# Two transformer blocks on one core: all attention issued beside projections, one score block ahead, and 64-row score matmuls issued in alternating pairs

## The reference

```python
# first block, mixer of one layer
a_in, b_x, b_b, b_c, q, k, v, gate_in = split_cols(h @ w_in[l], IN_SPLITS)
br_a = multiscale_pool(a_in, pool_w[l], pool_scale[l]) @ w_branch_a[l]
br_b = (b_b * causal_dwconv(b_c * b_x, conv_b_w[l])) @ w_branch_b[l]
q = apply_partial_rope(q.reshape(b, s, ATTN_HEADS, HEAD_DIM), cos, sin)   # 12 heads of 64
k = apply_partial_rope(k.reshape(b, s, ATTN_HEADS, HEAD_DIM), cos, sin)
br_c = dilated_attention(q, k, v) @ w_branch_c[l]       # 3 groups, one softmax over them
merged = gates[:, :, 0] * br_a + gates[:, :, 1] * br_b + gates[:, :, 2] * br_c
x = x + rmsnorm(merged @ w_out[l], norm_mix_post[l])
# memory attention, 4 heads of 128, 256 keys: softmax(q k^T / sqrt(128)) v
# second block, layer 0: 8 query heads and 2 key heads of 64 in a window, with a sink; and
outs = [einsum('bhqk,bkhd->bqhd', p[:, 0] - lam * p[:, 1], v) for p, (_, v) in zip(probs, kv_parts)]
# (4 heads, two softmax maps of 64 rows each, values 128 wide)
# second block, layer 1: 16 heads, scores over 64 + 32 rows, values 64 wide, 768 keys
```

## Time and profile before

| | |
|---|---|
| median of 3 runs | 4576.96 us (4574.52 to 4582.12) |
| the profiled execution's own time | 4583.58 us |
| its span | 4581.8 us |
| TensorE (PE) busy | 4184.2 us, 91% of the span |
| weight loads (PEld) | 3461.2 us, 76% |
| DVE, ACT, POOL busy | 1836.9, 1392.0, 1419.6 us |
| mean granted TensorE clock | 0.916 of full speed |

### The profile page before, as it was taken

How to read it: one execution, slowest core, us unless ns; L and a number is a source line. 1 busy time by engine, 2 the same in 40 slices (tenths; PEclk the granted TensorE clock), 3 DMA queues, 4 the chain that set the end, 5 groups by cost and what they waited for, 6 DMA issues and landing times.

```text
span 4581.8 us, 48460 instructions
## 1 busy us (share of the span) xinstructions
PE 4184.2 (91%) x19548; PEld 3461.2 (76%) x19548; DVE 1836.9 (40%) x3065; ACT 1392.0 (30%) x2044; POOL 1419.6 (31%) x644
## 2 busy tenths in 40 slices
PE   6899998999989999999988888889999879989998
PEld 4778767777668776767767777779999668876886
DVE  4433445654643243574454444341111544433113
ACT  3223334332322233433223333231111323343222
POOL 2213533655431254355541000112222200003442
PEclk9877999999997799999989988799999877789999
DMA  2211332444321133234431000012221100002332
GB/s 91 66 42 58 113 92 69 127 126 129 99 75 37 51 111 101 64 118 126 126 109 28 19 19 19 24 42 64 61 64 56 47 14 13 12 25 72 94 94 77
DMA packets 544827, 317.85 MB, mean 69 GB/s; under 512 B 35876, under 2 KB 517599, under 8 KB 544607
## 3 DMA queue, kind: packets, MB, share of 16 engines
q1 hardware_dynamic: 544335, 313.71, 23.4%
q10 hardware_dynamic: 272, 1.05, 0.1%
HBM read 312.62 MB, written 2.10 MB: 69 GB/s over the span
## 4 chain that ended last, share of the span: by engine, by line
PE 80%; DVE 12%; ACT 3%; issue 2%; POOL 1%; DMA 1%; SPq 0%; PEld 0%; DVEq 0%; PEldq 0%; ACTq 0%
PE acc L452 23%; PE acc L454 22%; PE acc L453 22%; PE ob L1058 3%; PE pt L1033 2%; PE ob L868 2%; PE ob L1310 2%; POOL wlo L436 1%; PE pt L862 1%; DVE small L1145 1%; DVE t L701 1%; DVE t L2169 1%; DVE t L592 1%; PE pt L688 1%; DVE hl L607 1%
## 5 line engine op out<-in xcount | busy, mean ns | idle before, releaser
L436 POOL TENSOR_TENSOR wlo<-wraw,whi 128x1024 fp32r<-128x1024 f32 (+5 forms) x640 | 1419.4, 2224 | 3126.6 <-ACT whi L429 3125.6
L452 PE MATMUL acc<-hh,whi 128*128 128x512 f32 (+4 forms) x3320 | 1297.6, 391 | 88.7 <-DVE hl L607 32.6
L454 PE MATMUL acc<-hh,wlo 128*128 128x512 f32 (+4 forms) x3320 | 1254.2, 378 | 0.0
L453 PE MATMUL acc<-hl,whi 128*128 128x512 f32 (+4 forms) x3320 | 1251.5, 377 | 0.0
L429 ACT ACTIVATE whi<-wraw 128x1024 fp32r<-128x1024 f32 (+5 forms) x640 | 625.0, 980 | 999.6 <-DMA wraw<-in_ada_w 269.0
L452 PEld LDWEIGHTS acc<-hh,whi 128*128 128x128 f32 (+1 forms) x3320 | 637.9, 192 | 243.2 <-issue 82.8
L453 PEld LDWEIGHTS acc<-hl,whi 128*128 128x128 f32 (+1 forms) x3320 | 638.3, 192 | 110.6 <-issue 17.9
L454 PEld LDWEIGHTS acc<-hh,wlo 128*128 128x128 f32 (+1 forms) x3320 | 636.1, 192 | 95.3 <-issue 0.2
L1439 DVE TENSOR_TENSOR t<-acc,sq 128x768 f32<-128x768 f32 (+1 forms) x44 | 36.3, 824 | 501.7 <-PE acc L454 501.7
L454 PE MATMUL acc<-act1h,wlo 128*128 128x512 f32 x528 | 209.5, 397 | 0.0
L1096 ACT ACTIVATE sq<-pt 128x768 f32<-128x768 f32 (+1 forms) x136 | 95.1, 699 | 375.2 <-PE pt L1033 375.1
(11 more groups left out here) (352 smaller groups left out, 6069.4 us busy)
## 6 DMA issues: line engine op xcount, KB each, us to landing
wraw<-in_ffn_w SPq DMA_DIRECT2D x120, 512.0 KB, 3.8
wraw<-in_w_in SPq DMA_DIRECT2D x102, 512.0 KB, 3.8
wraw<-in_ada_w SPq DMA_DIRECT2D x96, 512.0 KB, 4.0
wraw<-in_w_up SPq DMA_DIRECT2D x88, 512.0 KB, 4.0
wraw<-in_w_down SPq DMA_DIRECT2D x32, 512.0 KB, 4.3
wraw<-in_w_out SPq DMA_DIRECT2D x16, 512.0 KB, 4.0
wraw<-in_w_mkv SPq DMA_DIRECT2D x16, 512.0 KB, 4.0
wraw<-in_ab_w_in SPq DMA_DIRECT2D x14, 512.0 KB, 3.8
```

Source lines behind the costliest of these rows:

```text
L436: e.tensor_tensor(wlo[0:rows, s, a:b, 0:w], wraw[0:rows, s, a:b, 0:w], whi[0:rows, s, a:b, 0:w].bitcast(F32), ALU.subtract).then_inc(lo_re ...
L452: e.matmul(o, wh, xh, start=first, stop=False)
L453: e.matmul(o, wh, xl, start=False, stop=False)
L454: return e.matmul(o, wl, xh, start=False, stop=last)
```

## The change

The functions for attention alone, for attention beside projections, and for tiles of projections become one family, `pe_flow`, `act_flow` and `dve_flow`. It takes a list of iterations, a list of jobs (slabs and small steps with them) and a list of ticks, which says which part of which job runs in which iteration. Either list may be empty; with no iterations (`wide`) the jobs use the four slots of `acc0` and `acc1`. With iterations the scores take both `acc`, PV has `ob[0]` alone and the slab has `ob[1]`, one bank, so a slab for 768 tokens becomes one of 512 and one of 256. TensorE's order in tick n is: scores of n+1, transposes of a finished slab of values, transposes of n, PV of n-1, part of a slab.

Where a head is 64 rows wide (the first block, window attention, both maps of differential attention), two neighbours' score matmuls are issued in turn, one from partitions 0 to 63 and one from 64 to 127, into `acc0` and `acc1`:

```diff
+                if its[n].get("pair"):
+                    if n % 2:
+                        return
+                    side = [(n, 0), (n + 1, 0)]
+                for k, m in side:
+                    b = its[k]["s"][m]
+                    if used[b] is not None:
+                        masked, i = used[b]
+                        e.wait_ge(s_nb if masked else s_probs, c.at(s_nb if masked else s_probs, i + 1))
+                    used[b] = (its[k]["mask"] is not None, first[k] + m)
+                pieces = len(its[n]["maps"][0])
+                for p in range(pieces):
+                    for x in range(3):
+                        for k, m in side:
+                            q_hi, q_lo, k_hi, k_lo, at = its[k]["maps"][m][p]
+                            mm = e.matmul(scores_of(its[k], m)[:, at:at + k_hi.shape[-1]], q_lo if x == 2 else q_hi,
+                                          k_lo if x == 1 else k_hi, start=x == 0, stop=x == 2)
+                            if p == pieces - 1 and x == 2:
+                                mm.then_inc(s_scores, 1)
...
+            for n in range(-1, max(N + 1, len(ticks))):
+                tick = ticks[n + 1] if n + 1 < len(ticks) else None
+                over_ = jobs[before[0]] if ends(before) else dict(kind="")
+                vt = over_ if over_["kind"] in ("v", "kv") else None
+                raws += vt is not None
+                fulls += over_["kind"] in ("kv", "feat") or over_["kind"] == "plain" and not over_.get("rx")
+                if n + 1 < N:
+                    ready(its[n + 1]["need"])
+                    scores(n + 1)
+                if vt and not (wide and tick):
+                    values(vt)
+                if 0 <= n < N:
+                    t = its[n]
...
+                if 1 <= n <= N:
+                    t = its[n - 1]
+                    ready(t.get("need_v", t["need"]))
+                    e.wait_ge(s_copied, c.at(s_copied, n))
+                    e.wait_ge(ob_free[0], c.next(ob_free[0]))
+                    slot["pv"] = n
+                    for j, vj in enumerate(t["v"]):
+                        mm = e.matmul(ob[0][:, 0:t["dv"]], sq[:, 0, j * P:j * P + P], vj, start=j == 0,
+                                      stop=j == len(t["v"]) - 1)
+                    mm.then_inc(s_pv, 1)
                 if tick:
                     part(tick)
```

In a mixer of the first block pooling and convolution slabs move behind the slabs of queries, keys and values, beside the attention: 7 slabs with the 8 iterations of j = 0, 6 with those of j = 1. The loads on SP move with them:

```diff
-                ws, s = weights(e, c), c.turn("slab")
-                claim(e, c, s, TC)
-                take(e, c, [pt_free])
-                e.wait_ge(pool_ready, c.next(pool_ready, 4))
+                pe_flow(e, c, [], tiles_1(0), one_each(tiles_1(0)), hh, hl, wide=True)
+                pe_flow(e, c, its_1(0), jobs_1(0), ticks_1(0), hh, hl)
+                pe_flow(e, c, [], tiles_1(1), one_each(tiles_1(1)), hh, hl, wide=True, extra=(0, lambda: done_1(e, c, 0)))
+                pe_flow(e, c, its_1(1), jobs_1(1), ticks_1(1), hh, hl)
...
-                mm.then_inc(slab_done, 1)
-
-                for j in range(2):
-                    pe_tiles(e, c, tiles_1(j), K8, hh, hl)
-                    pe_attention(e, c, its_1(j))
-                    pe_features(e, c, ot1, 1, 4)
-                    feats = c.next(feat_ready, view="slab")
...
+                heads(0)
+                for g in range(4):
+                    load(e, c, [(0, P, rows_of(w_in, l, 0, KT, g * PG, PG))], PG)
+                conv(0)
+                heads(1)
+                conv(1)
+                conv(2)
```

The rotary turn is now a partition shuffle on DVE everywhere (before, only in the second block's streams); the matmul with the permutation is gone, and the lo part of tile i is taken by DVE before tile i+1's turn is begun. A convolution step or a pooling step is a job on DVE in its tick:

```diff
+                M, T, w, u = j["M"], j["T"], j["work"], j["t"]
+                src = jbank(s)[0:M, 0:T]
+                if j.get("rx"):
+                    st(e.tensor_tensor(j["raw"][0:M, 0:T], src, rstd[0:M, 0:T], ALU.mult))
+                    jrelease(e, s)
+                    src = j["raw"][0:M, 0:T]
+                e.tensor_tensor(w[0:M, 0:T], src, rope_c[0:M, 0:T], ALU.mult).then_inc(dve_step, 1)
+                e.stream_shuffle(u[0:M, 0:T], src, j["swap"]).then_inc(dve_step, 1)
+                e.wait_ge(dve_step, c.next(dve_step, 2))
+                if not j.get("rx"):
+                    jrelease(e, s)
+                st(e.tensor_tensor(u[0:M, 0:T], u[0:M, 0:T], rope_s[0:M, 0:T], ALU.mult))
+                e.tensor_tensor(w[0:M, 0:T], w[0:M, 0:T], u[0:M, 0:T], ALU.add).then_inc(s_sum, 1)
...
+                elif j["kind"] == "conv1":
+                    st(e.tensor_tensor(halves(zc[:, i % 2, PAD:]), halves(jbank(s)), bx(i), ALU.mult))
+                    jrelease(e, s)
+                    st(e.tensor_scalar(w, zc[:, i % 2, PAD:], wcol(2), None, ALU.mult))
+                    for k in (1, 0):
+                        st(e.scalar_tensor_tensor(out=w, in0=zc[:, i % 2, PAD - 2 + k:PAD + SEQ - 2 + k], scalar=wcol(k),
+                                                  in1=w, op0=ALU.mult, op1=ALU.add))
+                    st(e.tensor_tensor(w, w, rstd[:, 0:SEQ], ALU.mult))
```

More of the change, by code:

```diff
@@ L972, in instances, with ends @@
             return first, n
[L974 to L995 removed]
+        def ends(tick):
+            return tick and tick[3]
@@ L1000, in part @@
                 if k0 == 0:
[L1001 to L1009 removed]
+                    if t.get("fetch", True) and t["kind"] != "feat":
+                        slot["work"] = weights(e, c)
@@ new lines, in part @@
+                    slot["was"] = slot.get("s")
+                    if wide:
+                        slot["s"] = c.turn("slab")
+                        claim(e, c, slot["s"], SEQ)
+                    else:
+                        slot["s"] = None
+                        e.wait_ge(proj_free, c.next(proj_free))
+                    if t.get("stats"):
+                        e.wait_ge(pt_free, c.next(pt_free))
+                s = slot["s"]
+                if t["kind"] == "feat":
+                    e.wait_ge(ob_free[0], c.at(ob_free[0], 1 + t["after"] - slot.get("pv", 0)))
+                    for r in range(4):
+                        mm = e.transpose(jbank(s)[:, r * P:r * P + P], t["src"][:, r, :], ident[:, :])
+                    mm.then_inc(s_job, 1)
+                    return
@@ L1106, in act_stream @@
-                if tick and tick[3]:
-                    j = jobs[tick[0]]
-                    head(e, c)
-                    s, done = c.turn("acc"), c.next(slab_done)
-                    if j["kind"] != "rope":
-                        e.wait_ge(slab_done, done)
-                        e.activation(v3(sq[:, 1, 0:j["T"]], j["T"]), bank(s, j["T"], j["M"]), ACT.Copy).then_inc(s_raw, 1)
+                    if n == N:
+                        e.wait_ge(s_copied, c.next(s_copied, N))
+                        e.sem_inc(pt_free, 1)
@@ new lines, in act_flow @@
+                if n + 1 < N:
+                    exps(n + 1)
+                    combs += len(its[n + 1]["maps"]) == 2
+                if ends(before):
+                    j = jobs[before[0]]
+                    if j["kind"] in ("rope", "pool", "conv2") or j["kind"] == "plain" and j.get("rx"):
+                        sums += 1
+                        e.wait_ge(s_sum, c.at(s_sum, sums))
+                        e.activation(j["hi"], j.get("arrange", same)(j["work"][0:j["span"], 0:j["T"]]), ACT.Copy).then_inc(s_hi, 1)
@@ L1210, in dve_stream @@
+            before = None
+            for n in range(-1, max(N + 2, len(ticks))):
+                tick = ticks[n + 1] if n + 1 < len(ticks) else None
+                if n + 1 < N:
+                    for m in range(len(its[n + 1]["maps"])):
+                        maxima(n + 1, m)
+                if 0 <= n - 2 < N:
                     result(n - 2)
-                if before and before[3]:
+                if ends(before):
                     j, s = jobs[before[0]], slots[before[0]]
-                    if j["kind"] != "v":
+                    if j["kind"] in ("rope", "pool", "conv2") or j["kind"] == "plain" and j.get("rx"):
@@ L1645, in swap, with both @@
-        def swap(block, half):
-            return [p + half if p % block < half else p - half if p % block < 2 * half else p for p in range(32)]
+                         dst=otm[:, r, a * P:a * P + P], s=(r % 2,), need=needs[a][0], need_v=needs[a][1])
+                    for a in range(4) for r in range(4)]
+        all_tok = [slice(i * P, i * P + P) for i in range(4)]
+        def both(kind, hi, lo, **more):
+            return [dict(more, kind="rope", span=more["M"], T=SEQ, hi=hi[:, 0:SEQ], lo=lo[:, 0:SEQ], done=False),
+                    dict(more, kind="plain", span=more["M"], T=CTX, c0=SEQ, hi=hi[:, SEQ:TC], lo=lo[:, SEQ:TC], fetch=False)]
```

1042 lines of the change are left out of this document (437 added, 605 removed).

## The result

The changed kernel takes 4627.93 us (median of 4 runs, 4617.35 to 4629.0) against 4579.34 of the kernel before on the same chip: the ratio is 1.0102, 95% interval 1.0084 to 1.012. It is 1% slower, where 6% faster was forecast. Its profiled execution has a span of 4627.2 us.

What follows compares the result with a forecast made beforehand. TensorE, busy 91% of the span, was taken as the bound: its work divided by its clock. Gains 98 + 16 + 75 + 72 + 5 = 266 off 4583.6 gave 4317.6, less 6.6 about 4310 us; range 4200 to 4440.

Steps and rivals of the forecast that it cites:

- The two waits it has every iteration ... go: Differential attention, layer 0 of the second block: waits for ACT's exponential (0.73 us) and DVE's combination (0.44) vanish.
- The text's own warning: Sign of being wrong: DVE stands between TensorE and its accumulators in more than the rotary tiles; no size given.
- First-block mixers: Two first-block mixers: each falls from 341.9 to 292.7 us, a gain of 49, 98 for both.
- lateness of rotary tiles: First-block mixers: rotary tiles, paced by DVE and ACT, take 8.2 us each, 2.6 late; 18 us a mixer (4 to 24).
- Memory attention: Memory attention: its idle 8.2 us is covered by eight slabs that move in; 8 a layer, 16 gained (0 to 25).
- Layer 0: Second block's layer 0: window and differential attention fall from 433 us to 353 plus 5 of half clock; 75 gained (35 to 105).
- Layer 1: Second block's layer 1: a head falls from 23.9 to 18.3 us; less 13 for half clock, 72 gained (10 to 90).
- Small edges: The key tile and waits for slots: 5 us gained.
- F: Mixers' rotary tiles, pooling and convolution jobs: POOL stretches DVE's SBUF-only instructions, 283 us lost, about 4594; chance 0.07.
- D: Pairs overlap wholly, rotary tiles are not late, first block has no half clock: 105 us less, 4205; chance 0.12.
- B: Pairs of score matmuls on different row halves don't overlap: 16 us lost, 4325; chance 0.18.
- C: Half clock stays in the second block, a new wait of some 2 us a head sufficing: 99 us lost, about 4410; chance 0.19.

Runs made afterwards that it cites:

- early result: Changed kernel with DVE's result of an iteration moved ahead of the tick's slab job, from behind the next scores' maximum: 4352.83 us, ratio 0.9505.
- unpaired kernel with the early result: Kernel with the early result, a pair's scores issued one head or map after the other, not in turn: 4361.21 us, ratio 0.9521.
- lo part late: Early result, plus the lo part of the first block's wide rotary tiles taken behind the next tile's turn: 4326.63 us, ratio 0.9451.
- value transposes late: Early result, plus the transposes of a finished slab of values put behind those of the probabilities: 4392.33 us, ratio 0.9596.
- copy early: Early result and lo part late, plus ACT's copy of transposed probabilities moved ahead of the slab's rounding: 4359.49 us, ratio 0.9521.
- the kernel with the result one place earlier: Changed kernel with DVE's result ahead of the next scores' maximum, still behind the slab job: 4429.26 us, ratio 0.9677.

## Why the prediction was wrong

Its direction failed in one step of the changes in attention: "The two waits it has every iteration ... go", and for latent attention "Now the slab has a bank of its own, the scores are one ahead". I took the waits that this removes and put what it needs at nothing, TensorE's wait for PV's bank; it measured 242.9 us in 157 waits. PV has one bank, result(n-2) must be out of it before PV(n-1), and on DVE that result is queued behind the wait for scores of n+1, their maximum and a slab's job. The working even had DVE's pieces side by side and asked whether they fit into a tick by their sum. They do; DVE is busy 1827.0 us, 9.9 less than before. It was their order that mattered, and no sum of busy times shows it. The text's own warning, DVE between TensorE and its accumulators in more than the rotary tiles, is what came.

With that one line moved, 4352.8 us lies in the range, 43 from the forecast. Against the terms (windows with the early result against before):

- First-block mixers: 98 forecast, 57.1 + 65.3 = 122 found with the gates. The first mixer without them, before and with the early result:

```profile
54.70:392.35 337.65, 311.79 (x1261) 252.91 (x1259) 134.58 (x222) 92.47 (x121) 74.19 (x32) 0.80 0.17 49
...
55.00:332.60 277.60, 253.68 (x1268) 200.21 (x1267) 138.74 (x223) 87.77 (x118) 73.00 (x32) 0.93 0.19 56
```

  That is 60 for my 49. Half clock came out as forecast, 277.6 x 0.07 = 19 us for my 18. Mis-sized were the idle time, 23.9 us where I had 35 (8.7, 18 and 8), and the pairs, for which this term had nothing: the same stretch is 282.3 us long in the unpaired kernel with the early result. The lateness of rotary tiles was right in kind: 7.26 us a tile for my 8.2, and 20 us of it could be had back.
- Memory attention: 16 forecast, -1.0 + 3.4 = 2 found. The idle time was not covered: 12.3 and 12.1 us in these windows where it was 9.5 and 10.8, ACT's copy of the probabilities the largest wait within the attention (4.6 us in 7 waits in the first).
- Layer 0: 75 forecast, 69 found.
- Layer 1: 72 forecast, 47 found. Half clock stayed at 0.86, 51 us of the window, where I took off 13.
- Small edges: 5 forecast; outside these six windows the kernel is 5 slower.

So part of that nearness is luck: 24 us too little in the mixers stand against 55 too much in the other terms. The working also has slips that don't decide anything: a third of 12 is 4.0 and not 4.4, 273.18 to 273.60 is 0.42, the 60 and 26 of F are 63 and 28, and the last 6 of D's sum has no source.

The rivals. B, that pairs don't overlap, is false: starts 3 to 4 ns apart. D was right about the pairs and wrong in its other two conditions: the rotary tiles are late, and the mixers keep 19 us of half clock each. Whether its 27 us for whole overlap is right isn't shown, since even the unpaired kernel overlaps. The Trainium skill, "TensorE: Matmul & The Clock Gate", Part 3: Packing small matmuls — row/col tiling, says that matmuls on different row groups run concurrently; the trace agrees. What the same part says of weight loads, that one overlaps a running matmul only when its row group differs, the trace contradicts: in the kernel before, full-height loads of 0.19 us run beside full-height matmuls that start 0.18 apart (PE L453 at 2480.84, PEld L454 at 2480.85, PE L454 at 2481.02).

C must not be judged by the mean clock, which rose from 0.916 to 0.93 by way of the first block. In the second block, where C places it, half clock did stay. Length by what the clock lacks is 90 us in layer 0 and 52 in layer 1 of the changed kernel, 71 and 91 before (whole stages, wider than C's windows), and the forecast left 5 and 13. So C's mechanism is part of the loss, with PV's wait (2.82 us in the tick shown) as the new wait a head; its 99 us alone don't reach the 318 that the forecast missed by. Even with the early result the two stages keep 48 and 51 us of it, and two experiments in layer 1 lost 33 and 40 us with it. F named the right sign by the wrong mechanism. One of a turn's five instructions is stretched, 1.98 or 2.11 us for 0.69, and not four. The rule of the Trainium skill, "GPSIMD Engine Reference", 8. Key points, is borne out in kind. Its price here is no factor on the instruction: DVE's instruction ended 0.55 us behind POOL's, so it paid for what POOL had left, 1.3 to 1.4 us in these turns.

## What to carry to other kernels

When a buffer goes from two to one, find the instruction that frees it and read what stands ahead of it in its engine's queue, waits included; if it is a step that itself waits for what the other engine has only just issued, every iteration pays. Freeing steps come first, right where their input is done, unless they then wait there themselves: the copy on ACT, moved by this rule to where it waits for PV, lost 33 us. Busy shares and per-tick sums of an engine can't show this, the written order can, at no cost and before anything is run. And ask of each saved microsecond on one engine, as with pairs in layer 0, which engine sets the period then; and of an experiment that takes a mechanism away, whether the trace says that it is gone.

## What the runs showed of the hardware

- Two 64-row matmuls on the two halves of the rows, each with its own weight load, start 3 to 4 ns apart and take the time of one. With one map's six written behind the other's six, the second's first started at 2419.62, ahead of the first map's last three: across the halves the starts don't follow the written order.
- In layer 1 TensorE's clock differs between kernels with the same work, and none of the waits orders it. It was 0.86 and 0.88 with one wait a head of 1.3 us on average (early result; lo part late), and 0.78 with one of about 2.0 (value transposes late; copy early), at some 3 us more a head. But the changed kernel waited 68.4 us in 56 waits, up to 2.8, and had 0.88, and the kernel with the result one place earlier was at 0.91 with 50.8 us of idle time, where the two at 0.78 had 44.0 and 43.3:

```profile
3595.80:3959.60 363.80, 313.00 (x2003) 272.39 (x2001) 184.97 (x431) 162.79 (x314) 29.23 (x33) 0.91 0.07 18
```

  What does decide it isn't shown.
- A DVE instruction on a single column, both operands in SBUF, took 2.22 us while POOL worked and ended with POOL's instruction (2414.97 and 2414.96); its neighbour, with one operand of the same size, took 0.16:

```profile
2412.75 2.22 DVE L1012 TENSOR_TENSOR small<-small 128x1 f32<-128x1 f32 x1
2415.00 0.16 DVE L1014 RECIPROCAL small<-small 128x1 f32<-128x1 f32 x1
...
2411.98 2.98 POOL L443 TENSOR_TENSOR wlo<-wraw,whi 128x1024 fp32r<-128x1024 f32 x1 [15.69 <-ACT whi L436]
```
